# z, both gates, pa and pb as three fp32r products, with the attention output parked in DRAM

## The reference, cut to what matters

```python
qkv_a, z_a, a_a, b_a, q_b, k_b, v_b, g_a, g_b = split(rmsnorm(h) @ w_in)
o_a = gdn_finish(gated_delta(qkv_a, a_a, b_a), z_a)   # rmsnorm(o) * silu(z_a)
o_b = stick_breaking(q_b, k_b, v_b)                   # the sampled rows: over 2048 cached keys and values
m   = sigmoid(g_a) * (o_a @ w_pa) + sigmoid(g_b) * (o_b @ w_pb)
h   = h + m @ w_o
h   = h + (silu(gt) * up) @ w_ffn_out                 # gt, up = split(rmsnorm(h) @ w_ffn_in)
```

## Time and profile before

| | us |
|---|---|
| median of 3 runs | 1686.14 (1683.4 to 1686.49) |
| the profiled execution | 1687.39 |
| its span, first to last instruction | 1685.7 |
| PE busy in it | 1536.5 (91%) |
| mean granted TensorE clock | 0.941 of full |

### The profile page before, as it was taken

One profiled execution on the slowest core, in us unless ns is written; L12 is line 12 of the kernel. 1 busy time (PEld: TensorE's weight loads), 2 busy tenths in 40 slices (PEclk: granted clock), 3 DMA queues, 4 the chain that ended last, 5 costly groups with the idle time before them and its releaser, 6 DMA issues.

```text
span 1685.7 us, 24729 instructions
## 1 busy us (share of the span) xinstructions
PE 1536.5 (91%) x9226; PEld 1308.4 (78%) x9226; DVE 685.3 (41%) x2890; ACT 451.4 (27%) x644; POOL 137.9 (8%) x224
## 2 busy tenths in 40 slices
PE   6998996878999979788997999999898999999997
PEld 4876774556788769777874667668797999999996
DVE  2028655988876946541230000002325333332223
ACT  3011125643672333230111201110223222222122
POOL 0000001111211043201220000000000000000000
PEclk9999998998999988777898999999899999999998
DMA  3249773566655310005459899973131333332331
GB/s 105 63 147 327 261 242 140 188 196 217 225 175 161 99 29 8 7 1 174 127 153 304 303 305 296 314 238 126 50 88 53 98 88 96 93 89 81 91 91 51
DMA packets 236668, 248.69 MB, mean 148 GB/s; under 512 B 22329, under 2 KB 197571, under 8 KB 236517
## 3 DMA queue, kind: packets, MB, share of 16 engines
q1 hardware_dynamic: 236549, 247.12, 46.1%
HBM read 234.09 MB, written 13.19 MB: 147 GB/s over the span
## 4 chain that ended last, share of the span: by engine, by line
PE 76%; DVE 9%; DMA 5%; ACT 3%; POOL 2%; SPq 2%; issue 2%; POOLq 0%; DVEq 0%; ACTq 0%
PE ps L841 31%; PE ps L860 25%; PE ps L890 3%; DMA kring<-in_cache_k 2%; DVE kring L1749 2%; DMA vring<-in_cache_v 2%; PE ps L943 2%; PE ps L825 1%; PE ps L1222 1%; PE ps L1122 1%; PE ps L954 1%; PE ps L916 1%; SPq L609 1%; PE ps L1139 1%; PE ps L1112 1%
## 5 line engine op out<-in xcount | busy, mean ns | idle before, releaser
L841 PE MATMUL ps<-xn,wring 128*128 128x268 f32 (+2 forms) x2336 | 541.0, 392 | 6.5 <-DVE xn L1732 4.4
L841 PEld LDWEIGHTS ps<-xn,wring 128*128 128x128 f32 (+1 forms) x2336 | 443.3, 191 | 109.0 <-issue 29.1
L1749 DVE CUSTOM_DVE_ANT_0 kring<-kring,qv 128x128 f32<-128x128 f32 x1024 | 226.7, 290 | 43.0 <-DMA kring<-in_cache_k 42.9
L1372 ACT ACTIVATE R<-ps 128x520 f32<-128x520 f32 (+1 forms) x86 | 52.3, 609 | 507.0 <-PE ps L841 376.4
L482 DVE TENSOR_TENSOR wring_split<-wring,vring_split 128x1024 fp32r<-128x1024 f32 (+1 forms) x76 | 90.9, 1196 | 203.6 <-ACT vring_split L475 203.6
L860 PE MATMUL ps<-xn_split,vring_split 128*128 128x260 f32 x704 | 141.8, 283 | 8.2 <-DVE obT_split L496 8.1
L860 PE MATMUL ps<-obT_split,vring_split 128*128 128x260 f32 x704 | 142.2, 284 | 0.0
L860 PE MATMUL ps<-xn_split,wring_split 128*128 128x260 f32 x704 | 141.5, 283 | 0.0
L475 ACT ACTIVATE vring_split<-wring 128x1024 fp32r<-128x1024 f32 (+1 forms) x76 | 78.6, 1035 | 171.3 <-DMA wring<-in_w_ffn_out 103.0
L860 PEld LDWEIGHTS ps<-xn_split,vring_split 128*128 128x128 f32 x704 | 108.5, 189 | 9.5 <-issue 7.6
L860 PE MATMUL ps<-R_split,vring_split 128*128 128x260 f32 x592 | 111.1, 285 | 2.4 <-DVE rows_split L496 2.4
(11 more groups left out here) (350 smaller groups left out, 1812.7 us busy)
## 6 DMA issues: line engine op xcount, KB each, us to landing
kring<-in_cache_k SPq DMA_DIRECT2D x128, 512.0 KB, 4.8
wring<-in_w_in SPq DMA_DIRECT2D x72, 512.0 KB, 4.7
kring<-in_cache_v SPq DMA_DIRECT2D x68, 512.0 KB, 5.4
vring<-in_cache_v SPq DMA_DIRECT2D x60, 512.0 KB, 5.7
wring<-in_w_ffn_in SPq DMA_DIRECT2D x44, 512.0 KB, 3.8
wring<-in_w_ffn_out SPq DMA_DIRECT2D x16, 512.0 KB, 4.0
qv<-qdram SPq DMA_DIRECT2D x8, 512.0 KB, 6.2
out_rec_sample<-R SPq DMA_DIRECT2D x4, 1024.0 KB, 9.0
```

What stands on the lines that cost most here:

```text
L841: last = mm(ps[0:m, 2 * (t % 2) + i, 0:n], w_block(p, kk), src[:, k, a + i * n:a + i * n + n], start=(k == 0), stop=(k == n_k - 1))
L1372: go(halves(dst[:, first_token(t):TOKENS]), pair(t, m), func).then_inc(act_read, 1)
L1749: m = v.tensor_tensor_reduce(kh, kh, qbc[:, b % 2, h * P:h * P + P], 1.0, 0.0, ALU.mult, ALU.add, dz[:, b % 4, p * H + h:p * H + h + 1])
```

## The change

- Segments 7 and 8 change places: gB stands before pa. z, gA, gB, pa and pb are made by `tile_split`; the weight splits start at `FIRST_SPLIT`, the first z tile. Until `T_O` the high weight part has two slots in the old broadcast-q buffer (`w_high`), so `split_hi` of tile t+1 also waits for tile t-1 to be used.
- The normalised input is split in chunks 1 to 3 of `chunks()` (`gate_hi`, `gate_lo`, three, three and two rows). Its high part goes where `obT` lay. So at the end of segment 1 SP waits for the last head of the attention and stores `obT` to DRAM (`obdram`, 2 MB); behind the state stores it loads it again, to `obR`.
- The gated delta's output is split during gA, the attention output during pa; the samples' eight columns of it after the last `sum_v`, just before pb.
- V groups: ten stand in the z segment, two rings from the start, at tiles 41, 42, 43, 44, 44, 45, 45, 46, 46, 47; the other 22 stand one per tile in gA, gB and pa. Two samples are summed in the z segment. `vacc` keeps one buffer of the two.
- ACT's z read becomes three activations in place of one; its first waits for the store of the prompt's recurrent state. POOL's copy for the samples goes, and the masked keys are built by four instructions in place of one.
- Buffers move to fit; the work from `w_o` on is the same.

```diff
-SUMS_AT = {..., (6, 0): 5, (6, 5): 6, (8, 0): 7}
+SUMS_AT = {..., (6, 0): 5, (6, 4): 6, (7, 2): 7}
-QUAD_TILES = [8 * 5 + 2, 8 * 5 + 4, 8 * 5 + 6]
-QUAD_TILES += sorted([*range(8 * 6, 8 * 8 + 7), *range(8 * 6 + 2, 8 * 8 + 7, 4)])
+QUAD_TILES = [41, 42, 43, 44, 44, 45, 45, 46, 46, 47] + [i for i in range(8 * 6, 8 * 8 + 7) if i != 8 * 7 + 3]
...
+        def w_high(p, n):
+            return qbc2[:, p % 2, 0:n] if p < T_O else vring2[:, p % RING, 0:n]
...
+                if FIRST_SPLIT + 2 <= p < T_O:
+                    act.wait_ge(w_used, p - 1)
+                nc.scalar.activation(fr(w_high(p, n)), wring[:, p % RING, 0:n], ACT.Copy).then_inc(w_hi, 1)
...
# SP
-                if n == FIRST_LATE:
-                    sp.wait_ge(zs_done, 1)
-                    sp.wait_ge(t_dve, T_S0 + 16)
...
                         for i in range(4):
                             store_states(i)
+                        sp.dma_start(obR[:, :, META:LP], obdram[:, :, :]).then_inc(ob_in, 16)
...
+                if s == 1:
+                    sp.wait_ge(s_o, H)
+                    sp.dma_start(obdram[:, :, :], obT[:, :, META:LP]).then_inc(ob_out, 16)
...
# PE
+                    if s < 5:
+                        tile(T_SEG + s * KT + j, xn)
+                    elif s < 8:
+                        tile_split(T_SEG + s * KT + j, n_hi, n_lo)
+                    else:
+                        tile_split(T_SEG + s * KT + j, oa_hi, oa_lo)
+                    if s * KT + j in SUM_V_AT:
+                        if s == 5:
+                            pe.wait_ge(t_dve, T_S0 + 4 * (j - 4))
+                        sum_v(SUM_V_AT[s * KT + j])
+                        if s == 5:
+                            pe.wait_ge(ob_s, SUM_V_AT[s * KT + j] - V_EARLY + 1)
...
             pe.wait_ge(ob_s, DB - V_EARLY)
+            pe.wait_ge(g_lo, 3 * KT + 1)
             for n in range(KT):
-                tile(T_PB + n, obT)
+                tile_split(T_PB + n, ob_hi, ob_lo)
...
# ACT
+                    if 1 <= c <= 3:
+                        if c == 1:
+                            act.wait_ge(ob_out, 16)
+                        for k in range(3 * c - 3, min(3 * c, KT)):
+                            gate_hi(n_hi[k], n_full[k])
...
                     elif s == 5:
+                        if j == 0:
+                            act.wait_ge(r_out, 16)
                         if j >= 2:
                             act.wait_ge(z_done, j - 1)
+                        split_hi(act, t + 1)
+                        if t - T_SEG in SUM_V_AT:
+                            put_o(SUM_V_AT[t - T_SEG])
...
-                    elif s in (6, 8):
+                    elif s in (6, 7):
+                        split_hi(act, t + 1)
                         read_tile(t, (sgA if s == 6 else sgB)[:, j, :], ACT.Sigmoid)
+                        if s == 6:
+                            if j == 0:
+                                act.wait_ge(zs_done, 1)
+                                act.wait_ge(z_done, KT)
+                                act.wait_ge(r_out, 16 * 5)
+                            gate_hi(oa_hi[j], oa_full[j])
...
# DVE: in the samples' delta rule, and then for the segments 6 to 8
+                split_lo(dve, z)
                 step(v.tensor_tensor(bh(qk), of(0), of(1), ALU.mult))
                 step(v.tensor_copy(bh(kk), of(1)))
+                split_lo(dve, z + 1)
+                split_lo(dve, z + 2)
...
+            for s in (6, 7, 8):
+                for j in range(KT):
+                    t = T_SEG + s * KT + j
+                    split_lo(dve, t + 1)
+                    if (s, j) in SP_TILE:
+                        chain_sp(SP_TILE[s, j])
+                    if (s, j) in ARG_TILE:
+                        chain_arg(ARG_TILE[s, j])
+                    if s == 6:
+                        gate_lo(dve, KT + j, oa_hi[j], oa_full[j], oa_lo[j])
+                    if s == 8:
+                        gate_lo(dve, 2 * KT + j, ob_hi[j][:, 0:512], ob_full[j][:, 0:512], ob_lo[j][:, 0:512])
```

More of the change, by code:

```diff
@@ L180 @@
 N_QUAD = (DB - V_EARLY) * QUADS
-FIRST_LATE = 3
 def quad_ring(n):
-    return 1 if n < FIRST_LATE else (n - FIRST_LATE) % 2
+    return n % 2
 def quad_of(n):
@@ L206 @@
     _m = quad_before(_n)
-    if _n == 0:
-        _t = 8 * 5
-    elif _n == FIRST_LATE:
-        _t = 8 * 6
-    else:
-        _t = QUAD_TILES[_m] + 1
+    _t = 8 * 5 if _m is None else QUAD_TILES[_m] + 1
     QUAD_ISSUE.setdefault(max(_t, max(QUAD_ISSUE, default=0)), []).append(_n)
@@ L474, in split_hi @@
                 act.wait_ge(w_in_slot[p % RING], slot_value(p))
-                nc.scalar.activation(fr(whi[:, p % RING, 0:n]), wring[:, p % RING, 0:n], ACT.Copy).then_inc(w_hi, 1)
+                if FIRST_SPLIT + 2 <= p < T_O:
+                    act.wait_ge(w_used, p - 1)
+                nc.scalar.activation(fr(w_high(p, n)), wring[:, p % RING, 0:n], ACT.Copy).then_inc(w_hi, 1)
         def split_lo(dve, t):
@@ L490, in act_hi, with gate_hi, gate_lo, sampled_columns @@
                 act.wait_ge(dve_read, READ_COUNT[T_FI + 2 * (i - 2 * KT) + 1])
-            nc.scalar.activation(fr(kept(dst)), kept(src), ACT.Copy).then_inc(a_hi, 1)
+            nc.scalar.activation(fr(dst), src, ACT.Copy).then_inc(a_hi, 1)
         def act_lo(dve, i, hi, full, lo):
             dve.wait_ge(a_hi, i + 1)
-            nc.vector.tensor_tensor(fr(kept(lo)), kept(full), kept(hi), ALU.subtract).then_inc(a_lo, 1)
+            nc.vector.tensor_tensor(fr(lo), full, hi, ALU.subtract).then_inc(a_lo, 1)
+        def gate_hi(dst, src):
+            nc.scalar.activation(fr(dst), src, ACT.Copy).then_inc(g_hi, 1)
+        def gate_lo(dve, i, hi, full, lo):
+            dve.wait_ge(g_hi, i + 1)
+            nc.vector.tensor_tensor(fr(lo), full, hi, ALU.subtract).then_inc(g_lo, 1)
+        def sampled_columns(views):
+            return [v[:, KEPT - DB:KEPT] for v in views]
         def w_block(p, k):
@@ L901, in sum_v @@
                 for h in range(H):
-                    m = mm(ps[:, 5, h:h + 1], vacc[:, b % 2, h * P:h * P + P], selv[:, h:h + 1], start=True, stop=True)
+                    m = mm(ps[:, 5, h:h + 1], vacc[:, 0, h * P:h * P + P], selv[:, h:h + 1], start=True, stop=True)
                 m.then_inc(v_sum, 1)
@@ L1268, in _ @@
             for s in range(SEGS):
-                src = oaT if s == 7 else xn
-                if s == 7:
-                    pe.wait_ge(z_done, KT)
-                    pe.wait_ge(zs_done, 1)
+                if s == 5:
+                    pe.wait_ge(g_lo, KT)
+                if s == 8:
+                    pe.wait_ge(g_lo, 2 * KT)
                 if s == 6:
@@ L1658, in _ @@
                         sampled_out()
-                    if s * KT + j in SUM_V_AT:
+                    if s != 5 and s * KT + j in SUM_V_AT:
                         put_o(SUM_V_AT[s * KT + j])
@@ L1672, in _ @@
                     chunks()
+                    split_hi(act, FIRST_SPLIT)
             act.wait_ge(v_used, N_QUAD)
+            act.wait_ge(ob_s, DB - V_EARLY)
+            nc.scalar.activation(fr(obT2[:, :, LP:TOKENS]), obR[:, :, LP:TOKENS], ACT.Copy).then_inc(g_hi, 1)
             for n in range(KT):
+                if n + 1 < KT:
+                    split_hi(act, T_PB + n + 1)
                 act_hi(act, n, m_hi[n], m_full[n])
-                if n in (5, 6):
-                    split_hi(act, T_O + n - 5)
+                if n >= 6:
+                    split_hi(act, T_O + n - 6)
             copy_x(1, hT)
@@ L2051, in chunks @@
                         levels(c + 1)
+                    if 1 <= c <= 3:
+                        if c == 1:
+                            dve.wait_ge(w_used, done(T_SEG + 5 * KT - 1))
+                        for k in range(3 * c - 3, min(3 * c, KT)):
+                            gate_lo(dve, k, n_hi[k], n_full[k], n_lo[k])
             def sampled_delta():
@@ L2116, in _ @@
             log_decays()
-            for s in range(SEGS):
+            for s in range(5):
                 if s == 1:
```

148 lines of the change are left out of this document (85 added, 63 removed).

## The result

The changed kernel takes 1638.99 us, the median of four runs from 1635.9 to 1639.83. The kernel before takes 1684.77 us (four runs, 1680.95 to 1686.49). The ratio is 0.9728, 95% interval 0.9706 to 0.975. The profiled execution of the changed kernel has a span of 1638.1 us, and that of the kernel before one of 1685.7: 47.6 us less. Two later measurements, on two chips, gave 1642.8 and 1642.23 us for the changed kernel beside 1684.61 and 1685.81 us for the kernel before. They put the gain at 41.8 and 43.6 us, where this one puts it at 45.8.

What follows compares the result with a forecast made beforehand. PE's own work was taken as the bound, three quarters of the last chain. Terms -51.6 + 5.7 - 2.9 + 1.5 + 1 = -46.3 us took the profiled 1687.4 to 1641.1, median 1640 us; range 1626 to 1655.

Steps and rivals of the forecast that it cites:

- z: z stage: waits sum to +5.7 us; with seven more groups and two more sums, less eight tiles' gain, 118 us long.
- The product: z, gA, gB, pa and pb: each of 40 split tiles gains 1.29 us of PE, -51.6 us.
- The feed: ACT and DVE splitting weights and activations for the tiles: costed at nothing where ACT has only its reader.
- (b): z stage: ACT waits for the recurrent state's store before splitting tile 41's weight, +1.4 us.
- The large wait: Second group of gA: PE waits for V group 11, queued behind state stores and the attention output's load; 6 us.
- small V waits: gA to pa: density of transfers the same as before, so 6 us of small waits kept; bounds 0 and 14.
- second rival: The V waits go: group 11 early enough and small waits vanish, 14 us less, 1626 us; chance 0.18.
- (h): `chunks()`: three rows split per chunk; DVE lacks about 0.7 us in two chunks, +1.5 us, bounds 0 and 5.
- (i): End of the attention: SP stands still until its last head is copied, delaying queued loads; +1 us, 0 to 6.
- first rival: DMA becomes the bound of gA to pa: 223 us for the stage in place of 212, 1651 us; chance 0.14.
- rival of a late feed: Feed late at each tile: PE waits 2.6 us per tile, 52 us more, 1738 us; chance 0.04.
- the fourth: Splits bring less: products slower beside full DMA or K stage loses cover; 10 to 20 us less, about 1660; chance 0.06.

Runs made afterwards that it cites:

- e6_old_places: The changed kernel with the V groups behind the same tiles as before the change, still with two rings from the start: 1653.42 us.
- e2_two: The changed kernel without the product low weight by high activation in the 40 tiles from z to pb, the weight split still made: 1595.43 us (one run).
- e1_four: The changed kernel with a fourth product, low by low, in each of the 40 tiles from z to pb: 1712.23 us (one run).
- e4_early_split: The changed kernel with the first z weight split inside the last chunk in place of behind the convolution rows: 1641.42 us.
- e5_groups_between: The changed kernel with the V groups of tiles 45 and 47 between the sample's sum and the masked row steps: 1643.28 us.
- e8_park_alone: The kernel before with only the store and load back of the attention output added: 1690.42 us.
- e11_four_edits: The changed kernel with a later attention-output load, state store before convolution-row stores, and the edits of e4_early_split and e5_groups_between: 1636.21 us.

## Why the prediction was right

The forecast was 1640 us and the measurement 1639 (1642 to 1643 in the two later ones). The sum, in its own steps, with the profiled execution:

| step | predicted | measured |
|---|---|---|
| up to the end of the convolution rows | +2.5 | -3.5, -0.6, -1.1 |
| z | 118 | 125.9 from the end of the rows |
| gA, gB, pa | 212 | 208.8 |
| pb | 57.3 - 10.3 | 57.3 - 10.2 |
| behind pb | 0 | +0.4 |

**The product** was right. The readers of two pb tiles:

```profile
1108.26 0.70 DVE L2261 TENSOR_TENSOR R<-R,ps 128x520 f32<-128x520 f32 x1 [4.28 <-PE ps L883]
...
1113.99 0.70 DVE L2261 TENSOR_TENSOR R<-R,ps 128x520 f32<-128x520 f32 x1 [1.43 <-PE ps L883]
```

They stand 5.73 us apart, as those of `w_o` in the earlier trace rows. Beside V groups a tile takes 5.93 us, from the end of one group's matmuls at 970.38 to the next group at 976.31, as expected (5.91).

**The feed** was right: one wait for a low part in 40 tiles, and it is the one that was named.

**z** was predicted 7.4 us too short (the terms give 118.5). The first split's wait is 2.26 us (2.3 predicted), the two second groups wait 1.18 each (1.2), the sums 0.27 each (0.4). Tile 41 does not wait; the 1.4 us of (b) were taken by the slow clock of tile 40 (0.54 granted up to 773.4 us) in its place, as the last experiments show, and tiles 40 and 41 end within 0.3 us of where the sum had them. What failed is a step that the sum did not have: the clock. At full clock the second row step and the V group behind each of the two sums would take 2.12 and 1.85 us. They take 3.70 and 3.13 (852.14 to 858.97, and 6.84 together from 886.46 to 893.30), 2 x 2.9 = 5.8 us more, counted from start to start. The matmuls of the sampled step between tiles 41 and 42 take 23.9 us where they took 22.5, 1.4 more (0.58 granted in the first 23.6 us, 0.62 before from 785 to 808). Together 7.2. In the kernel before, a wide tile stood ahead of each pair of row steps, and the granted clock there was 1.00 (the stage 846 to 856 of the kernel before):

```profile
846.00:856.00 10.00, 9.68 (x58) 8.31 (x57) 4.31 (x16) 0.94 (x2) 5.02 (x3) 1.00 0.37 125
```

The change put two thin pieces of work behind each other, and I moved the sums in my account, but priced the work behind them at the clock of its old place. In every profiled execution of the changed kernel the clock falls at both sums (0.50 to 0.54 granted behind each); that the sums alone decide it is not shown, as e6_old_places says.

**gA to pa** was 3.2 us shorter than predicted. The large wait, its cause and its size were right:

```profile
914.30 3.64 PE L912 MATMUL ps<-kring,dw 128*32 128x512 f32 x16 [6.77 <-DMA kring<-in_cache_v]
```

and in SP's queue, the four stores of the states, the load of the attention output and the group's issue:

```profile
882.61 13.93 SPq L746 DMA_DIRECT2D out_rec_sample<-R  x4
896.59 4.20 SPq L766 DMA_DIRECT2D R<-obdram  x1
901.92 4.03 SPq L661 DMA_DIRECT2D kring<-in_cache_v  x4
```

From the first store to the pages 914.3 - 882.6 = 31.7 us, some 29 predicted; the wait 6.77, 6 predicted; the slow clock behind it about 2.7 (from start to start a group of 3.57 and a tile of 6.83 in place of 1.85 and 5.84; 0.50 and 0.84 granted), 2 predicted. No run shows the 2 us that stand in the sum of waits for this; what the changed kernel shows in their place is the 2.7. That the wait came so near is in part luck: the pages came 2 to 3 us later than predicted, and PE came 2.9 us later by the slow clock of the row steps and the group between 886.46 and 893.30 (0.54 granted). The small V waits were sized wrong: 6 us predicted, by the equal density of bytes, and there are none. Density was the wrong reading. What fits is two groups behind one tile, where the second has no tile to hide its transfer: the kernel before had 4.8 of its 6.4 us there, and e6_old_places, with the same split tiles and the double groups, has such waits again, 14.2 of 16.1 us at the second group. So half of the second rival came true (the small waits) and half did not (group 11). The chains of softplus and `cumulate` cost 0.80 + 0.90 = 1.7 us (3 predicted), and 1.7 more, which the sum did not have, go into a group at the slow clock (0.53 granted) behind the second. The wait ahead of pb is 0.92 (1 predicted).

**The early stages.** (h) and (i) cost nothing that can be seen. In a chunk PE takes 7.99 us from the first row to the second, in the changed kernel and in the kernel before:

```profile
692.42 1.04 PE L1202 MATMUL ps<-ident,qv 128*128 128x128 f32 x8
...
700.41 1.95 PE L1110 MATMUL ps<-tri_le,R 128*128 128x128 f32 x16
```
```profile
695.91 1.04 PE L1180 MATMUL ps<-ident,qv 128*128 128x128 f32 x8
...
703.90 1.95 PE L1088 MATMUL ps<-tri_le,R 128*128 128x128 f32 x16
```

DVE's idle time of 1.35 us was not all the room it had: the 0.7 us beyond it did not reach PE.

**The errors cancel**: +7.4 in z, -3.2 in gA to pa, and ahead of z between -3 and -6. So the range was the sounder statement, not the nearness of the one number. The first rival did not happen at three products (the second stage would be 223 us), but in e2_two, at two products, DMA has a share of 0.98 there. The rival of a late feed did not happen, and neither did the fourth. That PE sets the pace of the tiles rests on the readers in pb, on the group distances and on the readers in pb of e1_four; no run makes the three products without the rest of the change, and their worth of 51.6 us is the sum of such prices.

Not settled: why the stages ahead of z scatter by 2 to 3 us between executions of one kernel, what the fall of the clock in z depends on, and how e4_early_split, e5_groups_between, e8_park_alone and e11_four_edits come to stand to their neighbours differently by time and by stretch. Each stretch comes from one execution, and for the first three that one lies off the median.

## What to carry to other kernels

Price moved work at the clock of the place to which it goes: look what stands ahead of it, and if that is thin work or a wait, take the row of the same operation at the slow clock, where the record has one (here a row step of 3.78 us at 0.52 granted, 2.19 at 1.00). When a late transfer is the wait, look first at what its queue carries ahead of it, and ask for each piece whether someone wants it soon; moving one load of 2 MB to a later tile, and one store ahead of two others, brought 9.6 us by the medians and 7.1 in the stretch, where reordering PE's work brought nothing that the medians show. And when a wait is taken away, list the waits that end within the next few us: here the second one had been hidden by the first.

## What the runs showed of the hardware

The granted clock fell to about half without any long wait: 0.52 from 852.14 to 858.90 us, where PE had waited 0.27 and 0.32 us, but had run one-column sums and row steps. With V groups between, in e5_groups_between, the row steps kept the full clock (2.05 and 2.19 us, 1.00 granted), but the tile behind the second of these places ran at 0.51 for 5.7 us. The matmuls of the sampled step, of two columns each, ran at 0.58 for 23.6 us though PE was busy all the time:

```profile
783.00:806.60 23.60, 23.60 (x129) 23.52 (x128) 0.00 (x0) 1.73 (x4) 1.26 (x1) 0.58 1.06 337
```

The busy share of this row is 1 and its granted clock 0.58, so the share in the profile is not what to read the clock from: the granted clock is.

DMA held 337 GB/s for 190 us in e2_two, at a share of 0.98. The 354 GB/s that the prediction took as the rate at full share is not a ceiling: the earlier trace rows has 391 in a stretch of 4.3 us, and 20 us of e2_two moved more as well:

```profile
950.00:970.00 20.00, 17.55 (x145) 13.10 (x144) 4.38 (x4) 4.22 (x6) 0.00 (x0) 1.00 1.06 377
```
